# Queries and keys projected with features on partitions, in sixteen halves of the tokens, and two gate tiles moved ahead of attention

## What is computed

```
u = h @ p["w_in"]
q1, q2, k1, k2, v, z, xbc, dt = jnp.split(u, cuts, axis=-1)      # q, k: 256 columns each, 4 heads of 64
if rope is not None:                                             # latent tokens only
    q1, q2, k1, k2 = (apply_rope(t, cos, sin) for t in (q1, q2, k1, k2))
k_new = jnp.stack([k1, k2], axis=2)                              # output for the prompt tokens
o_a = diff_attention(q1, q2, k_all[:, :, 0], k_all[:, :, 1], v_all, lam)
y, hf, hb = bidir_ssd(xs, dt_f, dt_b, a[0], a[1], bm, cm, h0_f, h0_b)
y = rms_norm((y + d_skip * xs) * silu(z), ssm_norm_w)

def apply_rope(x, cos, sin):      # x1, x2: halves of a head's 64 features
    return concatenate([x1 * c - x2 * s, x2 * c + x1 * s], -1)
```

## Time and profile before

| | us |
|---|---|
| median of three runs | 1430.97 (1427.56 to 1431.09) |
| time of the profiled execution | 1428.95 |
| its span, first to last instruction | 1427.1 |
| PE busy | 1381.6 (97%) |
| DVE busy | 1059.5 (74%) |
| ACT busy | 546.8 (38%) |

### The profile page before, as it was taken

How to read it: one execution, slowest core, us unless ns; L and a number is a source line. 1 busy time by engine, 2 the same in 40 slices (tenths; PEclk the granted TensorE clock), 3 DMA queues, 4 the chain that set the end, 5 groups by cost and what they waited for, 6 DMA issues and landing times.

```text
span 1427.1 us, 22841 instructions
## 1 busy us (share of the span) xinstructions
PE 1381.6 (97%) x8704; PEld 1227.9 (86%) x8704; DVE 1059.5 (74%) x1695; ACT 546.8 (38%) x993; POOL 126.3 (9%) x221
## 2 busy tenths in 40 slices
PE   5999999999999999999999999999999999999996
PEld 3899988666889899899899889888989989989984
DVE  3695577776578888677677886777888867767778
ACT  4334462577255233233233254525533223323322
POOL 1300240112020101000000110002001100000011
PEclk9999999999999999999999999999999999999998
DMA  9712573798423343231232724632334423123141
GB/s 315 235 31 66 172 247 125 252 288 275 137 82 129 126 155 134 88 119 59 61 116 67 254 83 139 202 111 61 132 125 143 145 89 118 50 68 118 60 162 73
DMA packets 137004, 193.11 MB, mean 135 GB/s; under 512 B 5050, under 2 KB 105138, under 8 KB 136402
## 3 DMA queue, kind: packets, MB, share of 16 engines
q1 hardware_dynamic: 123250, 146.46, 32.0%
q0 software_dynamic: 12080, 42.41, 8.7%
q10 hardware_dynamic: 1584, 3.01, 0.6%
HBM read 177.30 MB, written 14.56 MB: 134 GB/s over the span
## 4 chain that ended last, share of the span: by engine, by line
PE 75%; DVE 10%; ACT 4%; issue 4%; DMA 3%; SPq 1%; POOL 1%; DVEq 0%; ACTq 0%; POOLq 0%
PE ps L858 37%; PE ps L1344 22%; PE ps L849 4%; PE ps L840 3%; PE ps L889 2%; DVE convT L2038 2%; PE ps L1152 2%; ACT h_full L1738 1%; DMA seg<-acs_rows 1%; SPq L576 1%; DVE p_pad L2699 1%; PE ps L1175 1%; DVE wlo L1942 1%; DMA raw_more<-in_w_mod_l 1%; ACT tmp L1738 1%
## 5 line engine op out<-in xcount | busy, mean ns | idle before, releaser
L1449 ACT ACTIVATE whi<-raw 128x512 fp32r<-128x512 f32 (+2 forms) x198 | 177.9, 907 | 358.8 <-PE ps L858 292.7
L858 PE MATMUL ps<-whi,hid_hi 128*128 128x512 f32 x640 | 249.6, 390 | 0.0
L858 PE MATMUL ps<-wlo,hid_hi 128*128 128x512 f32 x640 | 249.2, 389 | 0.0
L858 PE MATMUL ps<-whi,hid_lo 128*128 128x512 f32 x640 | 249.0, 389 | 0.0
L1942 DVE TENSOR_TENSOR wlo<-raw,whi 128x512 fp32r<-128x512 f32 (+2 forms) x198 | 204.1, 1038 | 24.3 <-ACT whi L1449 21.3
L2358 DVE TENSOR_TENSOR acc<-acc,ps 128x512 f32<-128x512 f32 x120 | 80.5, 685 | 111.3 <-PE ps L858 111.1
L858 PE MATMUL ps<-whi,h_hi 128*128 128x256 f32 (+1 forms) x440 | 146.0, 332 | 0.0
L858 PEld LDWEIGHTS ps<-whi,hid_lo 128*128 128x128 f32 x640 | 120.1, 188 | 25.3
L858 PEld LDWEIGHTS ps<-whi,hid_hi 128*128 128x128 f32 x640 | 120.1, 188 | 25.2 <-DVE wlo L1942 0.8
L858 PE MATMUL ps<-whi,h_lo 128*128 128x256 f32 (+1 forms) x440 | 141.6, 322 | 0.0
L858 PE MATMUL ps<-wlo,h_hi 128*128 128x256 f32 (+1 forms) x440 | 141.4, 321 | 0.0
(11 more groups left out here) (338 smaller groups left out, 2706.8 us busy)
## 6 DMA issues: line engine op xcount, KB each, us to landing
raw<-in_w_up_l SPq DMA_DIRECT2D x32, 1024.0 KB, 5.7
raw<-in_w_down_l SPq DMA_DIRECT2D x32, 1024.0 KB, 5.0
raw<-in_w_mod_l SPq DMA_DIRECT2D x26, 1024.0 KB, 6.3
raw<-in_w_in_l SPq DMA_DIRECT2D x12, 1024.0 KB, 5.3
raw_split<-in_w_mod_l SPq DMA_DIRECT2D x8, 1024.0 KB, 6.9
raw<-in_w_out_l SPq DMA_DIRECT2D x6, 1024.0 KB, 6.0
seg<-acs_rows POOLq DMA_DIRECT2D x10, 512.0 KB, 5.0
x_spill<-x_tok POOLq DMA_DIRECT2D x10, 512.0 KB, 5.1
```

The lines of the kernel that those rows point to most:

```text
L858: mm = pe.matmul(out, a_of(still, k), w_of(part, k), start=(first and k == 0 and part == 0 and still == 0), stop=(last and k == nk - 1 and ...
L1449: act.activation(ring_piece(whi, w, g), piece(w, g), ACT.Copy).then_inc(hi_done, 1)
```

## The change

- **q and k** are multiplied the other way round: 128 columns of weights (a pair of heads) are the weights of PE, and 320 of the 640 tokens move. Sixteen `project_qk(n)` of 24 matmuls take the place of twenty groups, in three PSUM banks (6, 4, 5). The results have features on partitions, so `turn_qk` and `evac_qk` are gone.
- **The rotation** (`rotate`) needs each feature's partner, now on another partition. A `stream_shuffle` swaps rows 16 apart within blocks of 32; for that, the columns of blocks 6 to 9 are put in another order while they are split (two or four strided pieces instead of one), and ACT puts the cached keys in that order (`kcp`). The table of cosines and sines grows to 128 x 1024 and is loaded after the cached keys have been transposed, since it takes their place.
- **The new keys** of the prompt, an output, are turned back by four transposes (`turn_new_k`, pair loop, step 9) and eight small copies on ACT.
- **z**: loop 1 has 8 halves, the pair loop 8 halves and z groups 0 and 1, ahead of the state loop is z group 2, in it 3 to 9. No z group is left in attention. The splits move: low parts of blocks 9 and 10 in steps 2 and 7 of the pair loop (3 and 8 before), high parts in 1 and 5 (2 and 7 before); z's first block is loaded one mod block sooner.

```
-    for c, n in ((3 * BW, 2), (C_Z, 3), (C_Z + BW, 2)):
+    for c, n in ((3 * BW, 2), (C_Z, 2), (C_Z + BW, 2)):
...
+            pool.wait_ge(kc_tr, 1)
+            pool.dma_start(rp[:], A["t_rope"].rearrange("p (a n) -> p a n", a=2)).then_inc(ld_small, 16)
...
+            def project_qk(n):
+
+                blk, hp, hf = n // 4, n // 2 % 2, n % 2
+                w = 6 + blk
+                if n % 4 == 0:
+                    pe.wait_ge(lo_done, 7 + blk)
+                if n < 3:
+                    pe.wait_ge(v_ev, (8, 9, 10)[n])
+                else:
+                    pe.wait_ge(qk_ev, n - 2)
...
+                half_still(bank(Q_BANK[n % 3], 0, HALF), features, h_cols(HP), hf, KT).then_inc(ib_mm, 1)
+
+            def project_z(z):
+
+                t = z % NT
+                if t == 0:
+                    pe.wait_ge(lo_done, 11 + z // NT)
+                if z < 2:
+                    pe.wait_ge(qk_ev, 14 + z)
+                else:
+                    pe.wait_ge(ib_ev, z - 1)
+                tokens_still(bank(4 + z % 2, 0, BW), h_tile(HP, t), w_cols(10 + z // NT, BW, 0, BW), KT).then_inc(ib_mm, 1)
...
-                project_in(4 * NT + j)
-                turn_qk(2 * NT + j - 1)
+                if j < 8:
+                    project_qk(8 + j)
+                else:
+                    project_z(j - 8)
+                if j == 9:
+                    turn_new_k()
                 site(j)
                 if j >= 1:
                     chunk_y(j - 1)
                 pair_products(j)
...
-                if a < 2:
-                    project_in(8 * NT - 2 + a)
...
+                    if in_rope_order(w):
+                        for a, u in quarter_turns(w):
+                            ins = dve.tensor_tensor(rope_order(ring_piece(wlo, w, g), a, u), natural(piece(w, g), a, u),
+                                                    rope_order(ring_piece(whi, w, g), a, u).bitcast(F32), ALU.subtract)
...
+            def rotate(n):
...
+                dve.wait_ge(ib_mm, V_DONE + n + 1)
+                mark(dve.stream_shuffle(u[:, 0:grid], src[:, 0:grid], [i ^ 16 for i in range(32)]))
+                mark(dve.scalar_tensor_tensor(dst, src[:, 0:grid], SCALE if blk < 2 else 1.0, rp[:, 0, t0:t0 + grid],
+                                              ALU.mult, ALU.mult))
+                if hf == 1:
+                    own = qT[:, 2 * blk + hp, LAT * P:TOK] if blk < 2 else kTp[:, 2 * blk - 4 + hp, :]
+                    mark(dve.tensor_scalar(own, src[:, grid:HALF], SCALE if blk < 2 else 1.0, None, ALU.mult))
                 settle()
...
+                mark(dve.scalar_tensor_tensor(u[:, 0:grid], u[:, 0:grid], SCALE if blk < 2 else 1.0, rp[:, 1, t0:t0 + grid],
+                                              ALU.mult, ALU.mult))
                 settle()
...
+                dve.tensor_tensor(dst, dst, u[:, 0:grid], ALU.add).then_inc(qk_ev, 1)
...
             for j in range(2 * NT):
                 if j >= 1:
                     weigh_pairs(j - 1)
-                evac_in(4 * NT + j)
-                if j in (3, 8):
-                    split_lo(9 + j // 8)
+                if j < 8:
+                    rotate(8 + j)
+                if j >= 9:
+                    evac_z(j - 9)
+                if j in (2, 7):
+                    split_lo(9 + j // 7)
                 if j >= 2 and j % 2 == 0:
                     chunk_sum(j // 2 - 1)
```

More of the change, by code:

```diff
@@ L68, in shape_tables @@
     sin = np.sin(ang).astype(np.float32).reshape(LAT, P, DH // 2)
-    rope = np.stack([cos, sin], 0).transpose(2, 1, 0, 3).reshape(P, -1)
+    feat = np.arange(DH).reshape(2, 2, DH // 4).transpose(1, 0, 2).reshape(-1)
+    side = np.where(feat < DH // 2, np.float32(-1), np.float32(1))
+    rope = np.stack([np.tile(cos.reshape(LAT * P, -1).T[feat % (DH // 2)], (2, 1)),
+                     np.tile(sin.reshape(LAT * P, -1).T[feat % (DH // 2)] * side[:, None], (2, 1))], 1).reshape(P, -1)
     icnt = np.zeros((4, PADW), np.float32)
@@ L486, in piece, with quarter_turns, natural, rope_order @@
             return (r[:, 0:4, 0:P], None, r[:, 0:4, P:BW], r[:, 4:8, 0:P], None, r[:, 4:8, P:BW])[g]
+        def quarter_turns(w):
+            if w % 2 == 0:
+                return [(None, u) for u in range(2)]
+            return [(a, u) for a in range(2) for u in range(2)]
+        def natural(ap, a, u):
+            if a is None:
+                return ap.rearrange("p (m u h f) -> p m u h f", u=2, h=2, f=16)[:, :, u]
+            return ap.rearrange("p (m a u h f) -> p m a u h f", a=2, u=2, h=2, f=16)[:, :, a, u]
+        def rope_order(ap, a, u):
+            if a is None:
+                return ap.rearrange("p (m h u f) -> p m h u f", u=2, h=2, f=16)[:, :, :, u]
+            return ap.rearrange("p (m a h u f) -> p m a h u f", a=2, u=2, h=2, f=16)[:, :, 1 - a, :, u]
+        def in_rope_order(w):
+            return 6 <= w < 10
         def ring_piece(buf, w, g):
@@ L1595, in _ @@
                     act.activation(dl, dx, ACT.Ln).then_inc(small_act, 1)
+                if g == 6:
+                    act.wait_ge(ld_old, 16 * 12)
+                    for u in range(2):
+                        ins = act.activation(kcp[:].rearrange("p t n h (a u f) -> p (t n h) a u f", a=2, u=2)[:, :, :, u],
+                                             kc[:].rearrange("p t n h (u a f) -> p (t n h) u a f", a=2, u=2)[:, :, u], ACT.Copy)
+                    ins.then_inc(kc_ok, 1)
                 if g == 8:
@@ L1600, in _ @@
                                        ACT.Copy).then_inc(kc_ev, 1)
[L1601 to L1608 removed]
+            for n in range(8):
+                if n % 4 == 0:
+                    split_hi(7 + n // 4)
+                if n == 2:
                     act.wait_ge(acs_ok, 3)
@@ L1619, in _ @@
                     site_store()
[L1620 to L1623 removed]
+                if j in (1, 5):
+                    split_hi(9 + j // 5)
+            tanh_z(1)
+            copy_new_k()
+            tanh_z(2)
             site_rows()
@@ L2156, in per_head, with evac_z @@
+            def evac_z(z):
+                t, half = z % NT, z // NT
+                dve.wait_ge(ib_z, z + 1)
+                dve.scalar_tensor_tensor(zs[:, t, half * BW:(half + 1) * BW], zth[:, z % 2, :], 1.0,
+                                         bank(4 + z % 2, 0, BW), ALU.add, ALU.mult).then_inc(ib_ev, 1)
             def per_head(ap, n):
@@ L2204, in _ @@
             dve.wait_ge(ld_small, 16 * 3)
-            for g in range(2 * NT, 4 * NT):
-                evac_in(g)
-                if g in (2 * NT + 2, 3 * NT + 2):
-                    split_lo(5 + g // NT)
-                if g == 2 * NT + 3:
+            for n in range(8):
+                rotate(n)
+                if n in (1, 5):
+                    split_lo(7 + n // 4)
+                if n == 3:
                     dve.wait_ge(dec_e, 3)
```

193 lines of the change are left out of this document (77 added, 116 removed).

## The result

The changed kernel took 1434.27 us, the median of 7 runs (1431.35 to 1435.54), against 1429.91 for the kernel before (7 runs). The ratio is 1.0033, with a 95% interval of 1.0021 to 1.0045: some 4.7 us slower by the ratio, 4.4 by the medians. The prediction said 1430.0, with 1427 to 1433 as the range of its likeliest case; only the wider range, up to 1435, takes in what was measured.

The account below looks back on a forecast made before the run. It took PE, with 75% of the chain, as the bound. -2.8 + 2.9 - 0.3 - 3.4 + 2.5 + 3.3 + 0.6 - 1.9 = +0.9 against 1428.95 gave 1429.9, forecast as 1430.0 us, range 1427 to 1433.

Parts of the forecast that it names:

- the two new waits: Pair loop, PE waits on DVE's low splits: step 3 before `chunk_y(2)`, +2.5 us; step 8 before z group 0, +3.3.
- attention without its z groups: Attention's steps 0 and 1 fall from 5.55 us to step 2's 4.53, less about 0.1: -1.9 us.
- Loop 1, -2.8: Loop 1: ten groups and nine turns become eight halves of 3.59 us each, -2.8 us.
- the old ones gone, -3.4: PE's three old waits for `weigh_pairs`, released by DVE, the largest before `chunk_y(8)`, go: -3.4 us.
- 5.3: Pair loop, forecast +5.3 us: +2.9 for changed matmuls and turns, -3.4 for old waits, +2.5 and +3.3 for new ones.
- From there to attention, +0.3: Between pair loop and attention: last turn goes, -0.3 us; state loop waits for block 11's split, +0.6.
- The pace of step 2: Attention's step 2, without a z group, took 4.53 us, set by the path through DVE and ACT, not by PE.
- cover for a wait: Attention's z groups covered a wait, so z's 5.9 us paid in the pair loop win back only a third there.
- become the bound of the pair loop: Rival, chance 0.15: strided or shuffled passes last twice as long, DVE bounds the pair loop, +6.7 us, 1436.6.
- Attention does not get shorter: Rival, chance 0.08: ACT's stores and copies ahead of the exponentials delay step 1's scores; -1.9 us is lost, 1431.8.

Follow-up runs that it names:

- Without the masks: Changed kernel with POOL's masks of pair 3 held until block 9's low split is done: 1432.47 us, ratio 1.0025 to the kernel before.
- split 9 first: Changed kernel with block 9's low split ahead of the rotation in step 2 of the pair loop: 1432.53 us, ratio 1.0021 to the kernel before.
- split 10 first: Changed kernel with block 10's low split ahead of the rotation in step 7 of the pair loop: 1432.64 us, ratio 1.0020 to the kernel before.
- the pair of kernels that differ only in the transposes: Changed kernel, z groups 8, 9 back in attention, block 9's split ahead of rotation; PE idle before z group 0: 1428.82 us; 22 unused transposes there: 1426.44 us.
- z back and split 9 first: Changed kernel with z groups 8 and 9 back in attention's steps 0 and 1, block 9's split ahead of the rotation: 1428.82 us, ratio 0.9992.

## Why the prediction was wrong

The step that failed is the price of a wait on PE. The prediction put the two new waits at +2.5 and +3.3, their lengths alone, and attention without its z groups at -1.9, all at the pace of the earlier trace rows, which are rows at full clock; it has no term for what PE's clock does behind a wait. Half clock cost some 1.5 us in the pair loop and 1.27 in attention, 2.8 of the 3.4 us by which the stages missed the forecast (+4.35 for +0.9). The profile before had a warning that I did not read: PE's wait of 2.25 us in front of layer 1, with 3.40 us at clock 0.50 behind it. The places, the releasers and the lengths of the waits it had right. Point by point:

- **Loop 1, -2.8:** -2.48. A half takes 3.60 to 3.63 us to the next row, not 3.59. Right, if 0.3 too hopeful. (One working beside the sum is off: 480 x 0.109 less 384 x 0.136 is 0.1, not 0.3. The sum doesn't use it.)
- **The waits, +2.5 and +3.3, the old ones gone, -3.4:** the places and releasers are as named, idle 2.57 and 2.79 us, and no other wait is left in the pair loop. Right in kind, and by their length together 0.2 less than forecast (5.6 for 5.8, with a matmul's own pace taken off each). That the first came out right was partly luck, for two errors offset each other: the split took 3.79 instead of some 2.8 us, as POOL's masks ran beside it, and the chunk sum's first pass 0.68 instead of the 1.12 of the earlier trace rows, where the masks still ran when it started. Without the masks the gap was 1.88.
- **What is missing in the pair loop:** 7.18 - 5.3 = 1.9 us. The z group behind the second wait runs from 204.98 to 209.30, 4.32 us for the 3.06 that it takes at full clock, and the site behind it 1.22 for 1.00. That is 1.5 of it. The rest, with the 0.2 by which the waits were shorter, is some 0.6; it is spread over the halves (3.63 for 3.59) and the changes between pieces, and was not tested.
- **From there to attention, +0.3:** +0.3, with 0.27 us idle before the group that uses block 11.
- **Attention, -1.9:** -0.65. The pace of step 2 was the right measure for step 0, and for step 1 at full clock (14.10 in the run with split 9 first). But z groups gone from there leave a wait of 2.10 us on PE, and half clock on the scores behind it, 1.27 us. The prediction called the groups "cover for a wait"; they were also cover for the clock.
- **From the stages to the median:** the profiled execution had half clock in two places beside the start and the end. The version with split 10 first had it for 6.8 us behind `chunk_y(2)` as well. The mean clocks of the seven runs are 0.988 to 0.991, and the profiled one has 0.991, so most had more of it. An estimate: 0.001 of mean clock over 1430 us is 2.9 us at half clock, or 1.4 us of work lost; before and after differ by 0.002 to 0.003, so by 3 to 4 us. That is the size of the error of 4.3 (1434.27 for 1430.0), but no more than that: the execution that is the median has 0.991 too and is 2.9 us longer than the profiled one, and no trace shows why.
- **The rivals:** DVE did not become the bound of the pair loop (41.14 of 57.93 us busy), and a rotation has its price: `rotate(10)` took 1.94 us for the 1.91 forecast, `rotate(15)` 1.60 for 1.60, with shuffles of 0.52 us for 320 columns and 0.37 for 192. "Attention does not get shorter" came partly true, but by another mechanism than ACT's order of work.

That the half clock comes from PE's idle time is shown by the pair of kernels that differ only in the transposes, in 23 executions and in their rows. When it follows a given wait isn't shown: the same wait in front of layer 1 had it in 6 of the 14 profiles and not in the rest. Nor do the single edits add up: split 10 first took away a wait with its half clock and won 1.9 us, where the same edit on the version with z back and split 9 first won 5.6.

## What to carry over

Price a wait on TensorE at its length and at what its clock does behind it: at gaps of 2 to 3 us here, another 1.3 to 2.4 us where the profile caught it, and nothing in some profiles. Look for waits in the profile before that have slower matmuls behind them, since curing one can win more than its length. Add up a change's terms for each version that you test: a gain larger than forecast is a reason to redo the sum. Work that seems to stand in the way of a stage may be what keeps TensorE busy while it waits for another engine; move it away only if what it covered goes as well. And look at the other engines' rows beside a stage's bottleneck: DVE's split cost half as much again because POOL's masks had come to lie beside it.

## What the runs showed of the hardware

- Matmuls of 256 columns started 0.12 us apart at clock 1.00 and 0.21 at 0.50, behind waits of 2 to 3 us. The low stretches there lasted 3.4 or 6.8 us. With PE busy in the wait up to 0.39 us before its end, the clock stayed at 1.00.
- DVE passes with both inputs in SBUF took longer beside POOL's mask instructions (3.79 for 2.49 us, 1.11 for 0.69, 0.79 for 0.36), and the masks 2.08 for 1.52. A split in one piece took 2.59 us beside masks that took 3.28. The pass `seg<-seg,ps`, with one input in PSUM, kept its 0.69 us.
- A stream shuffle from PSUM costs about what a copy does, 0.52 us for 320 columns and 0.37 for 192, and setting its mask 0.01. A low split in four pieces with runs of 16 elements cost 0.2 us more than in one pass.
